# Gate projections spread through the RWKV inverse, a split first input chunk, and sums moved between engines

## The chip, the cores and the metric

One Trainium2 chip, one of its cores. The metric is the device time of one execution in microseconds (us), from the runs' own counter. A core has five engines with instruction streams of their own: TensorE (PE, matmuls into PSUM), VectorE (DVE), ScalarE (ACT), GpSimd (POOL) and SyncE (SP, which here only starts transfers). They wait for each other by semaphores.

## What is computed

One layer of a hybrid decoder for 256 prompt rows and 8 sample rows, width 1024, float32. Shortened from the reference:

```python
mod = silu(c) @ w_mod + b_mod               # 6 x 1024 columns
sh1, sc1, gt1, sh2, sc2, gt2 = split(mod)
h = rms_norm(x, norm1) * (1 + sc1) + sh1
p = h @ w_in            # q | k | v | rwkv (1792) | gate_a (1024) | gate_b (1024)
o_a = sliding_window_attention(q, k, v)     # 8 query heads, 2 key heads
o_b = rwkv7_mix(p_rw)                       # delta-rule state, 8 heads of 64x64
m = sigmoid(gate_a) * (o_a @ w_pa) + sigmoid(gate_b) * (o_b @ w_pb)
x = x + gt1 * (m @ w_o)
x = x + gt2 * moe(rms_norm(x) * (1 + sc2) + sh2)   # top 4 of 32 experts
```

The recurrence over the 256 prompt rows is done in four chunks of 64 rows; each head and chunk needs the inverse of a triangular 64x64 matrix.

## The kernel before

Everything is kept transposed: 128 features on the partitions, T = 264 rows in the free dimension. A projection of 128 output columns is 8 matmuls of 128x128 by 128x264; in float32 each is two PE instructions, and each has its weight load. Weights come through a ring of six slots of 2 MB (`ring`), later with two more in `arena`.

**Transfers.** SP runs through the list `stream` with the slots of `slots_of`: four loads `modA` (the first 2048 columns of `w_mod`, two rows of 128 each), then input chunks (`win`, 512 columns each) and modulation chunks (`mod`) in turn, then `pa`, `pb`, `wo` and the last two `mod`. Before each reuse of a slot SP waits until PE has used it (`chunk_used`, which knows the order of PE's work by the list `a_order`). From `AFTER_RWKV` on it waits for the end of the carry (`carry_evac` 5). Behind the list come the experts' weights, 6 chunks of 2 MB for each of 32 experts (line 394).

**Setup.** PE turns x (line 837), adds up its squares over the partitions (831), makes scale and shift (855, 861); DVE forms `HT`, the normalised, scaled and shifted input (1550 to 1567), and PE starts input chunk 0 (909). Then for each pair: a modulation chunk (869, 875) and an input chunk (900).

**Gates.** Input chunks 5 to 7 and a quarter of 8 are 13 columns of the two gates. They are not worked off in one go: `gates(n)` in PE's stream (line 890) issues the next n of 104 steps (13 columns of 8 steps), at hand-chosen places where PE would wait. Each column has a PSUM bank from `GATE_BANK`; ACT takes it with `gates(b)` (557).

**Attention.** Four blocks `g4`: `scores` (986), softmax on DVE and ACT (1676 to 1685, 621), `probabilities` (transposes, 1000; ACT copies, 627) and `values` (1012). Then the sample rows' attention and state update, mostly on DVE (1697 to 1730).

**Inverse.** PE forms the triangular matrices (1129); DVE masks them (1759, 1761, 1764). Levels `i` of 1, 2, ..., 32 rows double the inverse: in each, PE makes Y (1156), ACT copies it (679), PE makes the corrections (1164, 1168), DVE adds them (1788, 1791), for two halves n. Keys by values (1176) and the product with the inverse (1185) follow, and then the carry: products over all heads and chunks (1202, 1205, 1209, 1210) and the state over four chunks (1219, DVE 1812 and 1814), output products (1225, 1226, 1229), the end state (1236).

**Rest.** Normalisation, mixer (1272), output projection (1304), router, and the experts (1359 to 1436).

## Time and profile before

| | |
|---|---|
| median of 3 runs | 1295.73 us (1293.49 to 1296.33) |
| profiled execution, its own time | 1295.52 us |
| its span, first to last instruction | 1293.7 us |
| busy: PE, PE weight load, DVE | 1243.3, 619.1, 446.1 us |
| busy: ACT, POOL | 296.8, 53.3 us |
| mean granted PE clock | 0.99 of 2.4 GHz |
| HBM read, written | 463.91 MB, 5.09 MB |

A busy time is the time in which at least one instruction of the engine ran. For PE it says little of how full the array is, since matmuls are pipelined. The idle time of an engine matters only where others wait for it. The chain of waits follows the last instruction back to what released it, step by step.

### The profile page before, as it was taken

Reading aid. Unit: us, or ns where it says so; the run is one execution under the profiler, and the core shown is the slowest. Engines: PE = TensorE matmul, PEld = TensorE weight load, DVE = VectorE, ACT = ScalarE, POOL = GpSimd, SP = SyncE. Lnnn points to the kernel's source line nnn. Section 1 sums busy time; section 2 is a strip of 40 time slices with the busy share of each in tenths; the row PEclk is TensorE's granted clock in tenths of the full one; section 3 lists DMA queues with packets and bytes.
Section 4 is the critical chain, followed back from the end, with each engine's and each line's share of the span. In section 5 each row is a group of like instructions: output and inputs, shape, how many; then the busy total and the mean of one; then the engine's idle time right before and its main releaser. Section 6 shows DMA issues by size and latency. Waiting matters only on the chain.

```text
span 1293.7 us, 21059 instructions
## 1 busy us (share of the span) xinstructions
PE 1243.3 (96%) x8371; PEld 619.1 (48%) x8371; DVE 446.1 (34%) x1035; ACT 296.8 (23%) x548; POOL 53.3 (4%) x67
## 2 busy tenths in 40 slices
PE   7999998899999999999999999999999999999998
PEld 5787786788743333333333333333333333333343
DVE  2145747546353222233322223332222223332232
ACT  3012441220232221122222112222211122221211
POOL 0010622200000000000000000000000000000000
PEclk9999998999999999999999999999999999999999
DMA  9976352148689999999999999999999999999995
GB/s 362 364 255 249 115 158 76 36 149 308 252 354 404 427 428 428 429 430 428 427 429 429 428 429 429 428 428 428 429 428 429 429 428 427 429 429 427 429 427 226
DMA packets 55613, 467.14 MB, mean 361 GB/s; under 512 B 5142, under 2 KB 7450, under 8 KB 29691
## 3 DMA queue, kind: packets, MB, share of 16 engines
q1 hardware_dynamic: 53354, 461.07, 85.9%
q0 software_dynamic: 1664, 5.20, 1.5%
q8 instruction: 40, 0.66, 0.2%
q10 hardware_dynamic: 544, 0.13, 0.0%
q14 instruction: 11, 0.08, 0.0%
HBM read 463.91 MB, written 5.09 MB: 363 GB/s over the span
## 4 chain that ended last, share of the span: by engine, by line
PE 77%; DMA 18%; ACT 2%; DVE 2%; issue 1%; SPq 0%; DVEq 0%
PE ps L1415 26%; DMA ring<-in_w 15%; PE ps L1436 14%; PE ps L1359 6%; PE ps L900 5%; PE ps L1384 4%; PE ps L890 4%; DMA ring<-in_w_in 2%; PE ps L1304 2%; PE ps L1272 2%; PE ps L1424 2%; PE ps L1366 1%; ACT PT L766 1%; PE ps L909 1%; PE ps L869 1%
## 5 line engine op out<-in xcount | busy, mean ns | idle before, releaser
L1415 PE MATMUL ps<-ring,PT 128*64 128x512 f32 x1536 | 337.3, 593 | 7.1 <-DMA ring<-in_w 6.8
L1970 DVE TENSOR_TENSOR SQ<-ps,SQ 128x528 f32<-128x528 f32 x124 | 79.1, 700 | 590.9 <-PE ps L1384 590.9
L1415 PEld LDWEIGHTS ps<-ring,PT 128*64 128x64 f32 x1536 | 109.8, 137 | 227.9 <-issue 210.4
L1436 PE MATMUL ps<-ring,PT 128*64 128x512 f32 x768 | 170.1, 595 | 0.0
L761 ACT COPY HT<-ps 128x512 f32<-128x512 f32 x62 | 33.3, 589 | 369.4 <-PE ps L1415 369.4
L1415 PE MATMUL ps<-arena,PT 128*64 128x512 f32 x512 | 113.5, 593 | 1.7 <-DMA arena<-in_w 1.7
L1436 PEld LDWEIGHTS ps<-ring,PT 128*64 128x64 f32 x768 | 53.2, 137 | 99.8 <-issue 99.8
L1359 PE MATMUL ps<-XR,PT 128*64 128x512 f32 (+1 forms) x384 | 94.1, 607 | 0.1
L1415 PEld LDWEIGHTS ps<-arena,PT 128*64 128x64 f32 x512 | 37.6, 137 | 74.0 <-issue 68.7
L1384 PE MATMUL ps<-PT 64*128 64x264 f32 x496 | 71.7, 408 | 0.0
L900 PE MATMUL ps<-HT,ring 128*128 128x264 f32 x304 | 69.3, 388 | 0.0
L774 ACT COPY PT<-ps 128x512 f32<-128x512 f32 x31 | 18.2, 587 | 199.7 <-PE ps L1436 199.7
L1384 PEld LDWEIGHTS ps<-PT 64*128 64x128 f32 x496 | 42.5, 185 | 41.4 <-issue 25.1
L900 PEld LDWEIGHTS ps<-HT,ring 128*128 128x128 f32 x304 | 57.3, 190 | 10.4 <-issue 0.8
L1436 PE MATMUL ps<-arena,PT 128*64 128x512 f32 x256 | 56.7, 595 | 0.0
L890 PE MATMUL ps<-HT,ring 128*128 128x264 f32 x208 | 53.4, 412 | 0.6 <-ACT arena L557 0.6
L890 PEld LDWEIGHTS ps<-HT,ring 128*128 128x128 f32 x208 | 40.9, 202 | 10.0 <-issue 2.7
L1359 PEld LDWEIGHTS ps<-XR,PT 128*64 128x64 f32 (+1 forms) x384 | 21.7, 134 | 49.6 <-issue 49.6
L761 ACT ACT_TABLE_LOAD x30 | 38.5, 1283 | 1.0 <-issue 0.5
L764 ACT ACT_TABLE_LOAD x30 | 38.5, 1283 | 0.5
L1424 PE MATMUL ps<-cst,HT 128*128 128x128 f32 x256 | 35.0, 280 | 0.7 <-ACT HT L787 0.7
L1932 DVE TENSOR_SCALAR PT<-cst,PT 128x128 f32<-128x128 f32 (+1 forms) x96 | 27.1, 339 | 24.8 <-DVE PT L1983 22.4
(457 smaller groups left out, 1154.8 us busy)
## 6 DMA issues: line engine op xcount, KB each, us to landing
ring<-in_w SPq DMA_DIRECT2D x144, 2048.0 KB, 27.1
arena<-in_w SPq DMA_DIRECT2D x48, 2048.0 KB, 27.7
ring<-in_w_mod SPq DMA_DIRECT2D x12, 2048.0 KB, 15.0
ring<-in_w_in SPq DMA_DIRECT2D x9, 2048.0 KB, 14.6
ring<-in_w_o SPq DMA_DIRECT2D x2, 2048.0 KB, 11.1
ring<-in_w_pa SPq DMA_DIRECT2D x1, 2048.0 KB, 9.1
ring<-in_w_pb SPq DMA_DIRECT2D x1, 2048.0 KB, 8.4
bias_rows<-bias_by_distance POOLq DMA_DIRECT2D x1, 1536.0 KB, 13.8
```

The source lines that it names most:

```text
L761: act.copy(UR[:, h, :].rearrange("p (f r) -> p f r", f=4), ps[:, 2 + h, :].rearrange("p (r f) -> p f r", f=4)).then_inc(sem["ur_evac"], 1)
L764: act.activation(US_, UG, ACT.Sigmoid, scale=1.702).then_inc(sem["us_ready"], 1)
L890: last = mm(ps[:, GATE_BANK[b], 0:T], w[:, k, s * P:s * P + P], HT[:, k, :], start=(k == 0), stop=(k == KD - 1))
L900: last = mm(bank[:, 0:T], w[:, k, s * P:s * P + P], HT[:, k, :], start=(k == 0), stop=(k == KD - 1))
L1272: last = mm(ps[:, k % 4, 0:T], w[:, i, k * P:k * P + P], (OA, OT)[q][:, i, :], start=(i == 0), stop=(i == 3))
L1359: last = mm(ps[64 * s:64 * s + 64, 0, :], OH[0:rows_in, n, :], XR[0:rows_in, n, s * 512:s * 512 + 512], start=(n == 0), stop=(n == 2))
L1384: last = mm(ps[:, bank + s, 0:T], YS[64 * s:64 * s + 64, p * P:p * P + P], GT[64 * s:64 * s + 64, :], start=True, stop=True)
L1415: last = mm(ps[64 * lin:64 * lin + 64, 2 + hh, :], XG[:, k % 4, k // 4, :], slot_tile(slot, c)[:, k % 2, lin * FE + hh * 512:lin * FE + hh ...
L1424: last = tr(ps[:, 2 + hh, f * P:f * P + P], UR[:, hh, f * P:f * P + P], ID)
L1436: last = mm(ps[64 * hh:64 * hh + 64, 4, :], AC[:, f, :], slot_tile(slot, c)[:, f % 4, hh * 512:hh * 512 + 512], start=(f == 0), stop=(f == ...
L1932: ins = v.tensor_scalar(OG[0:nt, n, :], IO2[0:nt, :], POSM[0:nt, n, col], GATE[0:nt, n, col], ALU.is_equal, ALU.mult)
L1970: v.tensor_tensor(YA[:, p::4, :], ps[:, bank:bank + 2, 0:T], YA[:, p::4, :], ALU.add).then_inc(sem["comb_used"], 1)
```

## The change

It has these parts:

- The four `modA` loads now hold first the scale columns (two loads of four rows of 128), then the shift columns; input chunk 0 is queued between them, in two loads of 1 MB. Input chunk 7 is queued behind modulation chunk 9 instead of ahead of it.
- The sums of squares for the first norm are made on ACT and DVE by rows (`accum_out`), and PE spreads the reciprocal roots over the partitions with three matmuls.
- Input chunk 0 is multiplied with the scaled, unshifted input (`SQ`); the shift vectors go through the same weights in 32 small matmuls, and DVE adds the result. `HT` with the shift is made for the later chunks.
- The scaling of the attention weights by their sums moves from DVE to ACT. The sample's queries are turned by two matmuls instead of eight.
- The 104 gate steps: 8 as before ahead of attention; 48 instead of 72 within it; 16 as before from there to level 1, at other places (4, 5, 4, 3 instead of 10, 4, 2); 12 instead of none in levels 2 to 5; 8 as before beside the product with the inverse; 12 instead of none in the carry. The columns get other PSUM banks.
- Keys by values are made in level 1 and copied there.
- Of the sample state's update a part moves from DVE's sample section into levels 1 to 4, and the sample output from the levels to behind level 5; the copy `OS` goes ahead of an addition.
- In the carry the pairs of products that add up in one bank are issued as two loops, first all of one kind and then all of the other; the output products go ahead of the state loop.

The core of the diff:

```diff
-        stream = [("modA", wmod, j) for j in range(4)]
-        for j, m in zip(range(5), (4, 5, 6, 7, 8)):
+        stream = [("modA", wmod, 0), ("modA", wmod, 1), ("win", win, 0), ("modA", wmod, 2), ("modA", wmod, 3), ("mod", wmod, 4)]
+        for j, m in zip(range(1, 5), (5, 6, 7, 8)):
             stream += [("win", win, j), ("mod", wmod, m)]
-        stream += [("win", win, 5), ("win", win, 6), ("win", win, 7), ("mod", wmod, 9), ("win", win, 8),
+        stream += [("win", win, 5), ("win", win, 6), ("mod", wmod, 9), ("win", win, 7), ("win", win, 8),
                    ("pa", None, 0), ("pb", None, 0), ("wo", wo, 0), ("wo", wo, 1), ("mod", wmod, 10), ("mod", wmod, 11)]
 
 
-        slots_of = [0, 1, 2, 3] + [4, 0, 1, 2, 3, 0, 1, 2, 0, 1] + [0, 1, 0, 1, 1, 0, 3, 2, 1, 4, 5]
+        slots_of = [0, 1, 4, 2, 3] + [0, 1, 2, 3, 0, 1, 2, 0, 1] + [0, 1, 0, 0, 1, 0, 3, 2, 1, 4, 5]
...
-        GATE_BANK = [4, 5, 7, 5, 7, 5, 7, 5, 7, 0, 3, 3, 2]
+        GATE_BANK = [4, 5, 7, 5, 7, 0, 7, 1, 3, 7, 3, 7, 0]
...
-                    sp.dma_start(row_pairs(slot), src[:, 2 * j:2 * j + 2, 0:2 * D]).then_inc(sem[f"ring{slot}"], 16)
+                    cols = slice(D, 2 * D) if j < 2 else slice(0, D)
+                    sp.dma_start(half_rows(slot), src[:, 4 * (j % 2):4 * (j % 2) + 4, cols]).then_inc(sem[f"ring{slot}"], 16)
+                elif (kind, j) == ("win", 0):
+                    sp.dma_start(ring[:, slot, 0:4, :], src[:, 0:4, 0:512]).then_inc(sem["ld_win0"], 16)
+                    sp.dma_start(ring[:, slot, 4:8, :], src[:, 4:8, 0:512]).then_inc(sem[f"ring{slot}"], 16)
...
+            def row_squares(n):
+
+                return act.activation(SQf[:, 0:D], XR[:, n, :], ACT.Square, accum_out=st[:, 70 + n:71 + n])
+
+            chain(row_squares(0))
             for k in range(KD):
-                chain(act.copy(XT[:, k, :], group()))
-                act.activation(SQ[:, k, :], XT[:, k, :], ACT.Square).then_inc(sem["a_evac"], 1)
+                act.copy(XT[:, k, :], group()).then_inc(sem["a_evac"], 1)
+            row_squares(1).then_inc(sem["ss_done"], 1)
             act.wait_ge(sem["ms_ready"], 1)
-            act.activation(RS[:, :], RS[:, :], ACT.Sqrt).then_inc(sem["sqrt_done"], 1)
+            act.activation(st[:, 70:73], st[:, 70:73], ACT.Sqrt).then_inc(sem["sqrt_done"], 1)
...
+                act.wait_ge(sem["att_sum"], g4 + 1)
+                for g in range(4):
+                    ins = act.mul(Pm[:, g, 0:J], Pm[:, g, 0:J], st[:, 8 + g:9 + g])
+                ins.then_inc(sem["att_p"], 1)
...
+                if i == 1:
+                    act.wait_ge(sem["u0_done"], 2)
+                    for n in range(2):
+                        for s in range(2):
+                            ins = act.copy(ZU[:, 8 * n:8 * n + 8, CH:P].rearrange("p (g s d) k -> p s g d k", s=2, d=2)[:, s],
+                                           ps[:, 3 + 4 * s, n * 256:n * 256 + 256].rearrange("p (g d k) -> p g d k", g=2, d=2))
+                        ins.then_inc(sem["u0_evac"], 1)
+                if i == 4:
+                    gates(9)
...
+            first_modulation(0)
+            pe.wait_ge(sem["ms_ready"], 2)
+            for n, (t0, nt) in enumerate(TILES):
+                last = mm(ps[:, 6, t0:t0 + nt], st[0:nt, 70 + n:71 + n].broadcast_to([nt, P]), ID[0:nt, 0:nt], start=True, stop=True)
+            last.then_inc(sem["ss_done"], 1)
+            first_modulation(1)
+            first_modulation_transposed(0)
...
+            def first_part(s, ks):
+
+                for k in ks:
+                    mm(ps[:, 4 + s, 0:T], w[:, k, s * P:s * P + P], SQ[:, k, :], start=(k == 0), stop=(k == KD - 1))
+
+            pe.wait_ge(sem["ld_win0"], 16)
+            for k in range(4):
+                pe.wait_ge(sem["h1_ready"], k + 1)
+                for s in range(4):
+                    first_part(s, [k])
+            weights("win", 0)
+            pe.wait_ge(sem["h1_ready"], KD)
+            first_part(0, range(4, KD))
+            first_modulation(2)
+            first_part(1, range(4, KD))
+            first_part(2, range(4, KD))
+            first_modulation(3)
+            first_part(3, range(4, 6))
+            first_modulation_transposed(1)
+            first_part(3, range(6, KD))
+            pe.wait_ge(sem["h1_ready"], KD + 1)
+            for k in range(KD):
+                for s in range(4):
+                    last = mm(ps[32 * s:32 * s + 32, 2, 2 * P:3 * P], SHT[:, k, :], w[:, k, s * P:s * P + P], start=(k == 0), stop=(k == KD - 1))
+            last.then_inc(sem["mod_a_used"], 1)
+            pe.wait_ge(sem["mod_a_evac"], 3)
+            tr(ps[:, 3, 2 * P:3 * P], MR, ID).then_inc(sem["setup_t"], 1)
 
             modulation(4)
+            pe.wait_ge(sem["h1_ready"], KD + 2)
+            pe.wait_ge(sem["setup_ready"], 2)
             project([1])
...
-            for h in range(HQ):
-                s = h % 2
-                last = mm(ps[:, 2 + s, NS * (h // 2):NS * (h // 2) + NS], II[64 * s:64 * s + 64, :], PTv[64 * s:64 * s + 64, h // 2, NP:T],
+            for s in range(2):
+                last = mm(ps[:, 2 + s, 0:4 * NS].rearrange("p (a b) -> p a b", b=NS), II[64 * s:64 * s + 64, :], PTv[64 * s:64 * s + 64, 0:4, NP:T],
...
             scores(0)
-            gates(12)
+            gates(8)
             pe.wait_ge(sem["qs_evac"], 1)
             scores(1)
-            gates(12)
+            gates(8)
             probabilities(0)
             scores(2)
             values(0)
-            gates(16)
+            gates(8)
             probabilities(1)
             scores(3)
             values(1)
-            gates(16)
+            gates(8)
+            pe.wait_ge(sem["att_max"], 3)
+            gates(3)
             probabilities(2)
             gates(1)
             values(2)
-            gates(12)
+            gates(10)
             probabilities(3)
-            gates(3)
+            gates(2)
             values(3)
...
-            gates(10)
+            gates(4)
...
-                    gates(4)
+                    gates(5)
...
-                if n == 0:
-                    gates(2)
+                gates(4 - n)
+            pe.wait_ge(sem["f_evac"], 8)
+
+            def keys_values(n):
+
+                for h, par in quads:
+                    u, q = 8 * n + h, other(h, par)
+                    col = 4 * n * CH + in_group(h) * CH
+                    last = mm(ps[64 * q:64 * q + 64, 7 if q != par else 3, col:col + CH], half(KR, par)[:, u, 0:CH],
+                              half(Vr, par)[:, u, :], start=True, stop=True)
+                last.then_inc(sem["u0_done"], 1)
...
+                if i == 1:
+                    pe.wait_ge(sem["f_evac"], 9)
+                    keys_values(0)
+                elif i == 2:
+                    pe.wait_ge(sem["u0_evac"], 2)
+                    gates(1)
+                else:
+                    gates(1)
...
+                    if n == 0:
+                        if i == 1:
+                            keys_values(1)
+                        else:
+                            gates(2)
...
             last.then_inc(sem["carry_done"], 1)
+            gates(2)
             for h, c in allu:
                 last = mm(head_chunk(4, h, c), rows_of(XZW, h, c, 0, CH), rows_of(Br, h, c, 0, CH), start=True, stop=True)
             last.then_inc(sem["carry_done"], 1)
-            pe.wait_ge(sem["f_evac"], GATES)
+            gates(2)
+
+            def first_in_bank(h, c):
+
+                return h < 2 and c < 2
+
+            def last_in_bank(h, c):
+
+                return h >= HQ - 2 and c >= NCHUNK - 2
+
+            pe.wait_ge(sem["f_evac"], 11)
             for h, c in allu:
-                mm(head_chunk(2, h, c), rows_of(Br, h, c, 0, CH), rows_of(XZW, h, c, CH, P), start=True, stop=False)
-                last = mm(head_chunk(2, h, c), rows_of(Kr, h, c, 0, CH), rows_of(Vr, h, c, 0, CH), start=False, stop=True)
+                mm(head_chunk(2, h, c), rows_of(Kr, h, c, 0, CH), rows_of(Vr, h, c, 0, CH), start=first_in_bank(h, c), stop=False)
+            pe.wait_ge(sem["dr_ready"], 2)
+            gates(1)
+            for h, c in allu:
+                last = mm(head_chunk(2, h, c), rows_of(Br, h, c, 0, CH), rows_of(XZW, h, c, CH, P), start=False, stop=last_in_bank(h, c))
             last.then_inc(sem["carry_done"], 1)
-            pe.wait_ge(sem["dr_ready"], 2)
+            gates(2)
             pe.wait_ge(sem["mc_ready"], 2)
-            for c in range(NCHUNK):
...
+            for h, c in allu:
+                mm(head_chunk(4, h, c), rows_of(Vr, h, c, 0, CH), rows_of(KR, h, c, CH, P), start=first_in_bank(h, c), stop=False)
+            gates(1)
+            for h, c in allu:
+                last = mm(head_chunk(4, h, c), rows_of(XZW, h, c, CH, P), rows_of(NR, h, c, CH, P), start=False, stop=last_in_bank(h, c))
+            last.then_inc(sem["o_done"], 1)
+            pe.wait_ge(sem["f_evac"], 12)
+            for c in range(1, NCHUNK):
+                pe.wait_ge(sem["g_ready"], c)
                 for h in range(HQ):
                     s, hp = h % 2, h // 2
-                    out = head_chunk(4, h, c)
-                    mm(out, rows_of(XZW, h, c, CH, P), rows_of(NR, h, c, CH, P), start=True, stop=False)
-                    last = mm(out, rows_of(Vr, h, c, 0, CH), rows_of(KR, h, c, CH, P), start=False, stop=True)
-                for h in range(HQ if c else 0):
+                    last = mm(ps[64 * s:64 * s + 64, 7, hp * CH:hp * CH + CH], MC[64 * s:64 * s + 64, hp, c, :],
+                              G4[64 * s:64 * s + 64, c - 1, hp, :], start=True, stop=True)
+                last.then_inc(sem["gm_done"], 1)
+                for h in range(HQ):
                     s, hp = h % 2, h // 2
                     last = mm(ps[64 * s:64 * s + 64, 6 if c < 3 else 3, (c - 1) % 2 * 256 + hp * CH:(c - 1) % 2 * 256 + hp * CH + CH],
                               G4[64 * s:64 * s + 64, c - 1, hp, :], ZR[64 * s:64 * s + 64, hp, c, 1, :], start=True, stop=True)
                 last.then_inc(sem["o_done"], 1)
+                gates(2 if c == 1 else 1)
...
+            def sample_state(part):
+
+                hs = slice(16 * (part % 2), 16 * (part % 2) + 16)
+                if part < 2:
+                    chain(v.tensor_tensor(T2[:, hs, :], sa[:, hs].unsqueeze(2).broadcast_to([P, 16, CH]),
+                                          VEC[:, 2, :].unsqueeze(1).broadcast_to([P, 16, CH]), ALU.mult))
+                elif part == 2:
+                    chain(v.tensor_tensor(S0[:, hs, :], S0[:, hs, :], T2[:, hs, :], ALU.add))
+                else:
+                    done(v.tensor_tensor(S0[:, hs, :], S0[:, hs, :], T2[:, hs, :], ALU.add), "smp_step", 1)
...
-                    sample_output(i - 1)
+                    sample_state(i - 1)
+            for part in range(4):
+                sample_output(part)
```

## Rows read from the trace of the kernel before

**Rows 1.** The page, part 2: transfer rate in 40 slices of 32.3 us.
```profile
GB/s 362 364 255 249 115 158 76 36 149 308 252 354 404 427 428 428 429 430 428 427 429 429 428 429 429 428 428 428 429 428 429 429 428 427 429 429 427 429 427 226
```

**Rows 2.** Chain of waits, whole span: start, length, engine, written tile, line.
```profile
362.10 2.97 PE ps L1359 x12
...
940.79 33.45 DMA ring<-in_w
...
999.55 33.42 DMA ring<-in_w
```

**Rows 3.** The same chain, setup.
```profile
34.70 14.50 PE ps L909 x64
...
51.09 14.44 PE ps L900 x64
```

**Rows 4.** Answer on line 358: issues (ns, first and last), transfers to landing.
```profile
L358 SPq DMA_DIRECT2D ring<-in_w_mod x4: 407/466/470, 3.5 to 5.0; - x4
...
DMA to landing us min/median/max: 10.0/16.8/24.3
```

**Rows 5.** Timeline of the setup: start, us, engine, line, operation.
```profile
20.20 1.28 ACT L544 ACT_TABLE_LOAD   x1
...
22.36 5.25 PE L855 MATMUL ps<-ring,cT 128*32 128x128 f32 x173
```

**Rows 6.** Timelines of projections and attention, DVE, ACT and POOL.
```profile
86.25 2.52 DVE L1588 SCALAR_TENSOR_TENSOR arena<-arena,PC,PT 128x264 f32<-128x264 f32 x6
...
133.00 0.36 ACT L597 COPY ring<-ps 128x256 f32<-128x256 f32 x1
...
146.86 4.70 DVE L1685 TENSOR_SCALAR ring<-ring,st 128x128 f32<-128x128 f32 x4
...
148.87 2.41 POOL L459 TENSOR_TENSOR PT<-ring 128x1024 f32<-128x1024 f32 x1
...
164.73 1.22 DVE L1678 TENSOR_REDUCE st<-ring 128x4 f32<-128x1028 f32 x1
...
166.20 0.51 ACT L621 ACTIVATE ring<-ring,st 128x257 f32<-128x257 f32 x1 [2.23 <-DVE st L1679]
```

**Rows 7.** Chain of waits from the sample's attention to level 1.
```profile
184.15 1.02 PE ps L1039 x8
...
199.85 2.30 DVE XR L1717
202.17 0.23 DVE XR L1719
...
203.09 5.84 PE ps L890 x16
...
209.49 1.13 PE ps L890 x4
...
220.44 0.69 PE ps L1156 x32
```

**Rows 8.** Busy time by stretch: engines (count), granted clock, DMA share, GB/s.
```profile
204.00:206.00 2.00, 2.00 (x6) 1.53 (x5) 1.83 (x6) 0.00 (x0) 0.00 (x0) 0.50 0.02 4
```

**Rows 9.** Chain of waits in the levels; PE's pauses of 120 to 290 us.
```profile
236.08 0.86 PE ps L1168 x30
...
242.35 2.32 issue
...
245.40 1.51 PE ps L1168 x30
...
250.67 0.52 PE ps L1176 x28
...
PE ps L1164 <- issue: 5.2, 4, 2.3
```

**Rows 10.** Chain of waits in the carry.
```profile
259.53 0.88 PE ps L1205 x60
...
272.31 3.76 PE ps L900 x16
```

More of the change, by code:

```diff
@@ L901, in project @@
                         last.then_inc(sem["a_done"], 1)
-            w = weights("win", 0)
-            for s in range(4):
-                bank = group()
-                for k in range(KD):
-                    if s == 0:
-                        pe.wait_ge(sem["h1_ready"], k + 1)
-                    last = mm(bank[:, 0:T], w[:, k, s * P:s * P + P], HT[:, k, :], start=(k == 0), stop=(k == KD - 1))
-                last.then_inc(sem["a_done"], 1)
+            w = ring[:, slots_of[STREAM_AT["win", 0]], :, :]
+            def first_part(s, ks):
[23 more added lines that the diff above has]
+            tr(ps[:, 3, 2 * P:3 * P], MR, ID).then_inc(sem["setup_t"], 1)
             modulation(4)
+            pe.wait_ge(sem["h1_ready"], KD + 2)
+            pe.wait_ge(sem["setup_ready"], 2)
             project([1])
```

162 lines of the change are left out of this document (79 added, 83 removed).

## The prediction

> **What bounds the kernel now.** I read the chain of waits over the whole span first. Its late part repeats two pieces: 33.45 us of waiting for an expert's weights at 940.79 and again at 999.55, so two experts take 58.76 us, 29.4 each [rows 2]. The transfer rate in forty slices is 427 to 429 GB/s from about 420 us on [rows 1]. So the end is set by the stream of expert weights, and that stream can't start before the ring slots come free, which TensorE (PE) decides: its first expert matmuls stand at 362.10 [rows 2]. Nothing in front of them is full for long: the slices before 300 us move 36 to 364 GB/s [rows 1]. What PE saves ahead of 362 us therefore moves the whole stream, and the end, by the same amount. The reader is to see two regimes: transfer bound behind, PE's own order in front.
>
> I then read the front in pieces: the setup, where PE waits for the first input chunk and starts it at 34.70 [rows 3]; attention and gates; the sample's attention; the inverse's levels; the carry. In each the question is whether PE works or waits.
>
> **Setup.** Before, four modulation loads and then the input chunk are queued; the first lands at 3.54 + 10.0 = 13.5, the last modulation load at 5.0 + 24.3 = 29.3, the chunk just before 34.70 [rows 3, 4]: 5.3 us per 2 MB. After, the same bytes come in another order: scale columns 13.5 and 18.8, chunk halves 21.5 and 24.1, shift columns 29.4 and 34.7, modulation 4 at 40.0, input chunk 1 at 45.3. The pieces are narrower (4 KB a row for modulation), which I take at the same rate.
> The row norms leave PE (eight 264-wide sums) for two 1024-wide squares on ScalarE (ACT); a table load of 1.28 [rows 5] and small instructions follow, and they should be ready near 17.7, before the second load lands. A modulation quarter is 64 matmuls at 5.25/173 us, 1.94 [rows 5]. So 18.8 + 1.94, then a copy, two transposes and four small VectorE (DVE) instructions at 0.23 [rows 7] and a first scaled row at 0.42 (2.52 for six) [rows 6], some 2.2 together: PE starts the chunk near 23.0. From there it owes the chunk, 14.5 [rows 3], two shift quarters, the shift pass and modulation 4 (4 x 1.94 = 7.8), and about 1.3 for two transposes with their copies: 23.0 + 23.6 = 46.6. The shift quarters are wanted at 32 and 38 and have landed. Final rows, 8 x 0.42 = 3.4 on DVE, lie under the shift pass and modulation 4; four copies out of PSUM with two small ones, near 2 in all, lie beside modulation 4. Chunk 1 landed at 45.3. It started at 51.09 before [rows 3]: **-4.5**. Bounds: 0 if cover fails everywhere, -5.8 if PE only waits for the landing.
>
> **Queries for the sample.** Eight small products become two wide ones, in front of the first scores: by the 64-wide instructions of the levels, 30 in 0.86 [rows 9], four instructions instead of sixteen save 0.4, by the wide steps' latency up to 1: **-0.7**. Bounds 0 and -1.
>
> **Attention.** Gate steps between scores and values fall from 72 to 48. A step is a pass like the 32 of the first chunk, 14.50/32 = 0.453 [rows 3], 0.46 with the change over, so 24 steps are 11.0 us off PE, if the softmax is still hidden. The scaling by the row sum moves from DVE to ACT: four 128x256 at 0.36 [rows 6] are 1.44 behind the exponentials. On DVE they took up to 4.70, because each waited out a GpSimd (POOL) instruction of 2.41 beside it [rows 6]. The wide softmax is then 1.22 (add) + 1.22 (max) + 0.2 + 4 x 0.51 + 0.3 + 1.44 = 6.4 [rows 6]. Its covers on PE: for the third block scores 1.1, values 0.6 and 11 steps (5.1), 6.8; for the fourth 11 steps and values, 6.9. Both hold by under 0.5. A DVE instruction caught behind POOL costs up to 2.4, once or twice in the first half. I take 0.7 of new waits: **-10.3**. Bounds: -11.0, and -6 with two such catches. PE's new wait for the third maximum has eight gate steps in front of it and should be free. In SP's queue modulation 9 now goes ahead of input chunk 7; both have 15 us or more before use, so nothing.
>
> **Sample's attention, up to the first products.** The chain from 184.15 is DVE's. The copy of the sample output goes ahead of the 2.30 us state addition at 199.85 [rows 7]; the outer product behind it goes to the levels. PE had then ten gate steps: 5.84 + 1.13 [rows 7] where ten cost 4.6, since the granted clock was 0.50 (1.2 GHz) at 204 to 206 [rows 8], after PE had waited for that copy. After: copy at 199.9 + 0.2, addition to 202.4, four copies to 203.2, with PE's four steps inside. The products start at 203.3 instead of 209.49 + 1.13 = 210.6 [rows 7]: **-7.3**. Bounds: -5 if a further DVE instruction comes in front, -7.5.
> Between there and level 1 five, four and three steps stand where four and two did: 12 against 6, 2.8 us, of which 0.9 falls into old waits for the masks: 11.7 instead of 9.8 (210.6 to 220.44): **+1.9**.
>
> **Levels.** They run from 220.44 to 250.67 [rows 7, 9], 30.2 us. PE's own work there is three blocks of 64 instructions a level, 1.4 to 1.8 each (30 in 0.86 [rows 9]), about 4.5, and 1.5 less in the last level: 21.0. The rest is waiting: for the evacuations by ACT, low clock, and pauses with no releaser, 5.2 us on one line, the largest 2.32 [rows 9]. Now 12 steps (5.5) and the keys-with-values (1.3, about 64 instructions) are put in those places: 21.0 + 6.8 = 27.8 if every pause goes. The sample state on DVE is again 1.22 per level, and DVE's 4.1 per level stays under PE's 5.9. **-2.4**. Bounds: -2.4, and +3 if the 5.2 of pauses stay.
> The pauses are where PE meets many 64x64 instructions. The largest fall where another transfer runs (the w_pa load, the state's store). By the Trainium skill (Runtime: NRT & Kernel Launch, Instruction fetch mechanics) the sequencer fetches instructions in blocks of 256 by DMA while the current block runs, mostly hidden. Taken so, longer gate instructions in between would hide it, and the whole sum would be 1273.1.
> The w_pa load is not gone: it waits for gate 11, which now ends in the carry, and its 2 MB land 9 us later, well before use but amid dense instructions. I add **+2.5** in levels and carry together for pauses that stay or move; bounds 0 and 7.
>
> **Level 5 to carry.** From 250.67 the keys-with-values (0.52 at their end) and their copies stood before the next product [rows 9]; both are gone from here: **-1.5**, and no less than -1 since that 0.52 and two ACT copies go. DVE gets four sample-output instructions (4 x 1.22 = 4.9) and 1.6 of bonus here, where PE has 7.2 with 8 steps: just covered; if not, +1.
> **Carry.** From 259.5 to 272.31 before [rows 10], 12.8. Twelve steps go in, 5.5. Some 3 of it covers waits: three times PE stood while DVE formed the next state (two instructions of about 0.45, by the 0.42 of rows 6), and once in a pause. About 15.2: **+2.4**. Bounds +1 and +5.
>
> **Sum.** -4.5 - 0.7 - 10.3 - 7.3 + 1.9 - 2.4 + 2.5 - 1.5 + 2.4 = -19.9. The first expert matmuls move from 362.1 to 342.2. The profiled execution took 1295.52 for a span of 1293.7; the median is 1295.73. 1295.52 - 19.9 = **1275.6**.
>
> **Rivals.** *A, the softmax becomes the bound* (chance 0.15): with ACT scaling, PE waits in each of three blocks some 1.5 to 2 more. For it: margins under 0.5. Against: DVE is relieved by up to 4.7. 1295.5 - 15 = 1281.
> *B, the pauses in the levels persist or grow* (0.15): 5.2 stays, the moved load adds 2 to 3: 1283.
> *C, the gates only change place* (0.04): total PE work is hardly less, so if waits come back elsewhere, 1293 to 1297, within 0.2%. Against it: PE stood idle for 2.32 in one pause alone [rows 9], and gates now stand there.
> *D, setup gains more and no pause stays* (0.10): 1295.5 - 24 = 1271.
> *E, slower* (0.03): PE's clock. At 244 to 248 level blocks went at 1.2 GHz, 1.51 against 0.86 for 30 instructions [rows 9]. Were the grant low from level 1 to the end of the carry, 45 us of work would grow by some 70%, 32 us: 1307. It decides from 28 us of such work on. Against it: lower grants lasted 3 to 7 us, and there are fewer gaps now. The Trainium skill (TensorE: Matmul & The Clock Gate, Part 1) says that idleness throttles and activity releases, which speaks for fewer drops.
>
> **Numbers.** My sum has 0.53. 0.2% is about what this kernel's measurement can tell from nothing. Faster is the forecast with A, B and D, 0.93; C gives 0.03 to same and 0.01 to slower: same 0.03, slower 0.04. The range runs from below D to above B: 1267 to 1286, and all but C, E and the tails of the others lie in it; its width is the bounds of attention (5), pauses (7), carry (4) and setup (4), not all at once.
>
> **What would show it.** Input chunk 1 starting near 46.6; last values of attention 15 us earlier; the first products after the sample's copies with no low clock in front; levels of 5.9 us with no pause over 1 us; first expert matmuls at 342; expert periods unchanged at 29.4. Wrong if attention shows PE waiting for ACT, if pauses move to the carry, or if the expert stream does not move along.

## The result

The changed kernel took 1282.23 us (median of 4 runs, 1281.01 to 1283.18) beside 1294.61 us for the kernel before (1291.26 to 1296.33, 4 runs): ratio 0.9901, 95% interval 0.9886 to 0.9916. Faster, as forecast, and inside the range, but by some 12 to 13 us where the sum had 19.9. The profiled execution took 1282.87 us for a span of 1281.0, 12.7 less than the span before.

The page, part 2, in 40 slices of 32.0 us, and the whole chain of waits of the changed kernel:

```profile
GB/s 356 367 286 249 101 104 70 101 294 305 222 347 428 426 430 427 428 430 427 428 429 428 428 429 428 428 429 428 428 429 428 428 429 428 428 429 426 429 428 222
...
347.30 2.97 PE ps L1440 x12
...
928.06 33.46 DMA ring<-in_w
986.84 33.44 DMA ring<-in_w
```

The two regimes are as before [rows 1, 2]. Two experts take 986.84 - 928.06 = 58.78 us, and the waits for their weights stand 12.73 earlier than the 940.79 of [rows 2]; the end moved with them. The first expert products stand at 347.30, 14.8 earlier than 362.10. So the front (all that PE does ahead of its first expert product) gave 14.8, not 19.9, and 2.1 were lost again behind 347 us. Setup, in the chain:

```profile
14.88 3.57 PE ps L871 x64
...
19.41 1.93 PE ps L871 x64
...
23.75 9.14 PE ps L934 x40
...
47.34 4.69 PE ps L926 x20
```

L871 is the first modulation, 64 matmuls a quarter: the first quarter took 3.57, the second 1.93. L926 is the second input chunk, 47.34 against 51.09 [rows 3]: -3.75. The sample's attention to level 1, in the chain, and below it busy time by stretch (the number behind the engines is the granted clock):

```profile
169.99 1.02 PE ps L1089 x8
...
186.60 3.82 PE ps L916 x8
190.43 2.84 PE ps L1179 x64
...
195.70 1.91 PE ps L1179 x64
...
203.12 1.09 PE ps L1216 x64
```

```profile
186.00:188.00 2.00, 2.00 (x7) 1.64 (x8) 2.00 (x1) 0.49 (x1) 0.00 (x0) 0.50 0.01 4
...
190.00:192.00 2.00, 2.00 (x33) 1.64 (x36) 0.00 (x0) 0.00 (x0) 0.00 (x0) 0.50 0.00 0
```

L916 are gate steps, two instructions each. Eight of them (four steps) took 3.82 at 186.60 at a granted clock of 0.50 (1.2 GHz, "the half clock" below) and 1.98 at 198.53, 233.12 and 236.14; the first 64 products (L1179) took 2.84, the next 64 only 1.91. Levels and carry, in the chain ("issue" is a pause for which the profile names no releaser):

```profile
201.59 1.53 PE ps L916 x6
...
207.30 0.89 issue
...
211.47 0.55 issue
...
228.36 0.64 PE ps L916 x2
...
230.08 1.09 PE ps L916 x4
...
232.25 0.88 PE ps L1249 x30
233.12 1.98 PE ps L916 x8
...
238.12 1.14 PE ps L1266 x62
...
250.20 1.73 issue
...
257.55 3.76 PE ps L926 x16
```

The gate groups of 1, 2, 3 and 4 steps took 0.64, 1.09, 1.53 and 1.98: 0.445 a step, and 0.19 for each group whatever its size. The start of the experts:

```profile
354.00:356.00 2.00, 2.00 (x6) 0.51 (x4) 0.88 (x4) 0.43 (x1) 0.21 (x1) 0.50 0.64 274
```

```profile
352.34 15.65 PE ps L1496 x64
```

The first 64 expert products ran partly at the half clock and took 15.65; in the run of the best version, below, they took 13.95.

### The profile page after: what moved, and what is told of

Its sections match the earlier page's. It is cut to its first block, busy times and chain, and to the rows that moved or that the text cites. A ratio compares the mean times of both kernels' runs of the same rounds, so it can differ in the third digit from the quotient of the medians.

```text
span 1281.0 us, 21166 instructions
## 1 busy us (share of the span) xinstructions
PE 1237.6 (97%) x8414; PEld 607.5 (47%) x8414; DVE 443.1 (35%) x1041; ACT 298.5 (23%) x558; POOL 53.0 (4%) x67
## 4 chain that ended last, share of the span: by engine, by line
PE 76%; DMA 16%; DVE 4%; ACT 3%; issue 1%; SPq 0%; POOL 0%; DVEq 0%
PE ps L1496 27%; DMA ring<-in_w 16%; PE ps L1517 14%; PE ps L1440 6%; PE ps L926 5%; PE ps L1465 4%; PE ps L1385 2%; PE ps L1353 2%; PE ps L916 2%; PE ps L1505 2%; PE ps L1447 1%; ACT PT L789 1%; PE ps L934 1%; PE ps L895 1%; PE ps L871 1%
## 5 line engine op out<-in xcount | busy, mean ns | idle before, releaser
L926 PE MATMUL ps<-HT,ring 128*128 128x264 f32 x304 | 69.3, 388 | 0.2 <-issue 0.2
L926 PEld LDWEIGHTS ps<-HT,ring 128*128 128x128 f32 x304 | 57.3, 190 | 10.7 <-issue 1.1
L916 PE MATMUL ps<-HT,ring 128*128 128x264 f32 x208 | 55.9, 410 | 0.0
L916 PEld LDWEIGHTS ps<-HT,ring 128*128 128x128 f32 x208 | 38.1, 195 | 8.1 <-issue 1.4
L784 ACT ACT_TABLE_LOAD x30 | 38.5, 1283 | 1.0 <-issue 0.5
L787 ACT ACT_TABLE_LOAD x30 | 38.5, 1283 | 0.5
```

What stands on the lines that cost most here:

```text
L784: act.copy(UR[:, h, :].rearrange("p (f r) -> p f r", f=4), ps[:, 2 + h, :].rearrange("p (r f) -> p f r", f=4)).then_inc(sem["ur_evac"], 1)
L787: act.activation(US_, UG, ACT.Sigmoid, scale=1.702).then_inc(sem["us_ready"], 1)
L916: last = mm(ps[:, GATE_BANK[b], 0:T], w[:, k, s * P:s * P + P], HT[:, k, :], start=(k == 0), stop=(k == KD - 1))
L926: last = mm(bank[:, 0:T], w[:, k, s * P:s * P + P], HT[:, k, :], start=(k == 0), stop=(k == KD - 1))
```

## The experiments

All were timed in five rounds; ratios are to the kernel before, run beside them. Each has one trace. "Attention" below is the time from the second input chunk's start to the sample's transposes behind the last values (before: 184.15 - 51.09 = 133.1; changed: 169.99 - 47.34 = 122.65).

**The changed kernel again** (no edit).

> The changed kernel itself once more, unedited, as the measure for the experiments beside it and for how far its profile repeats. Theory 1 (its first trace, with a mean granted clock of 0.995 and no half clock near 128, was a lucky execution; the experiments' own traces of the same attention code show the half clock at 124 to 132): more runs give a median 0.5 to 2 us above 1282.23, runs at a lower mean clock are the longer ones by some 0.8 us for each 0.001, and the stretch from the second chunk to the sample's transposes takes 123 to 126 us in place of 122.6. Theory 2 (the trace is typical): median within 0.5 us of 1282.2, clock 0.995, the stretch 122.6.

1285.29 us (1281.48 to 1286.83, 6 runs), ratio 0.9916 [0.9901, 0.9932] with before at 1295.78. The first theory holds in its direction: the first trace was a lucky execution. Its size was too small, since the median rose by 3.1 us where it had 0.5 to 2 (by the ratios it is 1.9, and the two intervals overlap). Over the ten executions of this kernel, six with a mean granted clock of 0.994 to 0.996 took 1281.0 to 1283.2 us, and four with 0.991 to 0.993 took 1283.9 to 1286.8. Attention took 123.3, with the half clock at 124 to 132 that the first trace lacks; the kernel before has one at 128 to 136. The half clock also followed the carry's pause, in the chain and by stretch:

```profile
251.41 1.75 issue
```

```profile
254.00:256.00 2.00, 2.00 (x32) 1.62 (x32) 0.23 (x1) 0.00 (x0) 0.00 (x0) 0.69 0.03 8
256.00:258.00 2.00, 2.00 (x20) 1.20 (x17) 0.62 (x2) 0.00 (x0) 0.00 (x0) 0.50 0.00 0
```

**Setup alone** (the kernel before with the setup part of the diff, its stream order included).

> The kernel before with the setup part of the change alone: first chunk in two loads without its shift, the split first modulation, the mean squares by row, and the stream order that these need; attention, sample, inverse and carry are those of before. Theory 1 (the setup's gain passes through whole): the second chunk's products start at 47.3 in place of 51.09, as in the changed kernel, every later mark is 3.7 to 3.8 us earlier, and the median is 3.8 us below before, ratio 0.997. Theory 2 (the gain is lost at the first wait of attention, whose softmax on VectorE and ScalarE sets the pace): the mark stands at 47.3, but the last values end less than 2 us earlier than 184.15 and the time is 0 to 2 us lower. What is left between this run and the changed kernel, 8.6 us by theory 1, is the worth of the rest of the change.

1292.82 us beside 1295.3, ratio 0.9975 [0.9963, 0.9987], 3.2 us (1.7 to 4.8) by the ratio. The second chunk started at 48.4 in its trace, and attention took 133.1 as before: the gain passes through attention whole. Over all traces with this setup code that start lies between 47.2 and 48.6, before it was 51.1 and 51.3, so the setup is worth 2.5 to 4.1. Its trace also warns of single traces: 2.6 us were gained at the end of attention, but 6.1 at the first expert products, though the code between is that of before. Those 3.5 us are the spread between executions.

**Gate steps ahead of the sample's wait.**

```diff
             token_rows(6)
             token_rows(7)
+            pe.wait_ge(sem["row_evac"], 6)
+            gates(4)
             pe.wait_ge(sem["smp_att"], 4)
...
             pe.wait_ge(sem["row_evac"], 8)
-            gates(4)
```

> The changed kernel with the four gate steps at 186.60 moved ahead of the wait for the sample's five copies (the wait for token rows' sixth copy goes with them), so that TensorE has work while VectorE copies from 185 to 189. Theory 1 (the low clock from 186 to 192 follows the light work ahead of it, and the four steps stood behind the idle time at half rate): the four steps take 1.98 us as at the full clock and not 3.82, they lie under VectorE's copies, the first 64-row products run at 1.91 us for 64 and not 2.84, level 1 starts 2 to 3 us earlier than 203.12, and the time falls by 2 to 3 us. Theory 2 (the clock falls here for another reason, or VectorE's copies, which end at 189.06, set the start of the first products): the first products start 0 to 0.5 us earlier than 190.43, the clock row still shows 0.50 in 187:190, and the time is within 0.7 us of the changed kernel.

1284.02 us, ratio 0.9908 [0.9889, 0.9927]: not to be told from the changed kernel. My first theory falls, and its picture with it. In the chain:

```profile
187.28 2.96 PE ps L916 x8
190.24 0.36 PE ps L1149 x4
...
192.00 1.05 PE ps L1180 x29
```

TensorE was not idle at the new place. The steps now stand ahead of L1149, which VectorE's last four copies need, and delay them; in the changed kernel they run beside these copies. The steps still met the half clock (2.96 for eight instructions). The products started 21.0 us after the last values' transposes, 20.4 in the changed kernel.

**Scaling of the attention weights back on VectorE**, in all blocks, and in all but the first.

```diff
-                v.reciprocal(st[:, 8:12], st[:, 8:12]).then_inc(sem["att_sum"], 1)
+                chain(v.reciprocal(st[:, 8:12], st[:, 8:12]))
+                for g in range(4):
+                    ins = v.tensor_scalar(Pm[:, g, 0:J], Pm[:, g, 0:J], st[:, 8 + g:9 + g], None, ALU.mult)
```

> The changed kernel with the scaling of the softmax weights back on VectorE, as before (four multiplications behind the reciprocal in place of ScalarE's). Theory 1 (ScalarE's four multiplications of 1.28 to 1.71 us a block are what TensorE waits for: 2.5 us of its idle time in attention and 0.3 more stand behind them): the weights are ready sooner, the last values end 1 to 2.5 us earlier than 169.99, and the time falls by as much. Theory 2 (VectorE is the fuller engine, and its multiplications behind GpSimd's instructions take 2 us and more, as the 4.70 us one did before): the last values end 2 us or more later than 169.99, and the time rises by 2 to 5 us. Theory 3 (either engine is as late as the other): within 1 us.

> The changed kernel with the softmax scaling on ScalarE for the first block of attention alone, and on VectorE for the other three. With all four on VectorE only the first block's multiplication was slow (4.69 us for four, behind GpSimd's instructions, TensorE idle 2.32 us); with all four on ScalarE TensorE idled 2.5 us in four waits of 0.3 to 0.9 us. Theory 1 (each wait is local, and no other wait takes its place): TensorE's idle time ahead of these transposes falls to 0.9 us or less, and the stretch to the sample's transposes is 1.2 to 1.8 us shorter than in the changed kernel at the same clock. Theory 2 (VectorE's own chain is as full, and its sinks and copies come later by as much): idle time only moves to the score or value products, under 0.5 us of gain.

All blocks: 1286.37 us, ratio 0.9932 [0.9917, 0.9947], attention 126.1. All but the first: 1284.0 us (1281.44 to 1289.2), ratio 0.9906 [0.9892, 0.9921], attention 127.1. The changed kernel's waits, and the multiplications in the timelines of the two runs, one fence each:

```profile
PE ps L1048 <- ACT ring L641: 2.5, 4, 0.9
```

```profile
143.44 2.42 POOL L458 TENSOR_TENSOR ring<-ring,arena 128x1056 f32<-128x1056 f32 x1
143.93 4.69 DVE L1789 TENSOR_SCALAR ring<-ring,st 128x128 f32<-128x128 f32 x4
148.67 0.66 PE L1044 MATMUL ps<-cst,ring 128*128 128x128 f32 x4 [2.32 <-DVE ring L1789]
```

```profile
148.80 2.21 DVE L1789 TENSOR_SCALAR st<-st 128x4 f32<-128x4 f32 x1
153.01 3.17 DVE L1798 TENSOR_SCALAR ring<-ring,st 128x128 f32<-128x128 f32 x4
```

On VectorE the multiplications that fall beside GpSimd's 2.4 us instructions (143 to 156) were slow, and so was a small one ahead of them: four elements a partition took 2.21. With the first block's scaling on ScalarE the second was caught, and TensorE idled 3.6 for it. But not all of that is the scaling's: the small one was also caught with all scaling on ScalarE, in the traces of the merged groups, the paired sums and the late load below, where TensorE idled 1.7 to 1.8 and attention took 126.0, 126.0 and 124.7. From the first of them:

```profile
148.83 2.20 DVE L1782 TENSOR_SCALAR st<-st 128x4 f32<-128x4 f32 x1
154.36 0.66 PE L1048 MATMUL ps<-cst,ring 128*128 128x128 f32 x4 [1.71 <-ACT ring L641]
```

So the traces show which instruction waits, but the length of attention alone doesn't tell the engines apart, and neither does the time: both intervals overlap that of the changed kernel's second set. Both of my readings of single waits were too local. From 155 us on GpSimd has many short instructions instead of those; the best version below takes VectorE in the last two blocks, and its trace has none of these waits.

**The same gate steps in seven groups fewer.**

```diff
                 elif i == 2:
                     pe.wait_ge(sem["u0_evac"], 2)
-                    gates(1)
+                    gates(3)
                 else:
-                    gates(1)
+                    gates(3)
...
-                        else:
-                            gates(2)
```

> The changed kernel with the same gate steps in fewer groups: three steps at once in each of levels 2 to 5 in place of one and two, and in the carry 4, 4, 2, 1, 1 in place of 2, 2, 1, 2, 1, 2, 1, 1. Seven groups fewer. Theory 1 (each group of full-width products between 64-row products costs a fixed 0.18 us, as the groups of 1 to 12 steps show: 0.64, 1.09, 1.53, 1.98 and 5.54 us): TensorE loses 7 x 0.18 = 1.3 us, and if no wait opens in the levels the time falls by 1.0 to 1.3 us. Theory 2 (the spread groups hide waits for VectorE's copies in the levels): TensorE idles between the halves of a level for 0.3 us or more each, and the time rises by 0.5 to 2 us. Theory 3: the two cancel, within 0.5 us, with both to be seen in the trace.

1283.21 us (1279.38 to 1286.37), ratio 0.9899 [0.9880, 0.9918]; not to be told from the changed kernel by time. Its profiled execution was the longest of its six. The traces tell more: from level 1 to the product with the inverse 27.8 us instead of 29.1 in both traces of the changed kernel, for four groups fewer and pauses of 1.2 against 1.4 and 1.2. That is 1.3 where 4 x 0.19 gives 0.76, so the price of a group fits only roughly. In the carry the pause grew instead, and the half clock followed (chain):

```profile
251.26 2.77 issue
...
254.72 2.06 PE ps L916 x4
```

**The load of `w_pa` kept back.**

```diff
+                if kind == "pa":
+                    sp.wait_ge(sem["carry_evac"], 5)
```

> The changed kernel with the 2 MB load of the first output-side matrix kept back until the carry's fifth copy, some 15 us later, so that no large transfer is under way in the carry. Theory 1 (TensorE's pause of 1.73 us at 250.20, for which the trace names no wait, is an instruction fetch held up behind that load; before, the pause of 1.77 us at 222.40 stood behind the same load): the pause shrinks to 0.6 us or less or is gone, and the second part of the last chunk starts 1.1 to 1.7 us earlier, at 255.9 to 256.4 in place of 257.55; the time falls by that or, if the matrix is now late, less. Theory 2 (the pause is one of the regular fetches of this many short instructions and has nothing to do with the load): it stays at 1.5 us or more, at the same place in the instruction stream, time unchanged within 0.5 us. A cost: the product with that matrix may wait for it; then a wait on its ring slot shows.

1281.77 us (1278.89 to 1283.14), ratio 0.9889 [0.9874, 0.9903], beside 0.9916 [0.9901, 0.9932] for the unedited one run with it: the medians are 3.5 us apart, but the intervals touch, and beside the first four executions (1282.23) it is 0.5. What the edit does is read from the trace. By stretch, the changed kernel first (the last two numbers are the transfer share and GB/s):

```profile
248.00:250.00 2.00, 2.00 (x90) 1.71 (x89) 0.00 (x0) 0.00 (x0) 0.00 (x0) 1.00 0.74 299
250.00:252.00 2.00, 0.27 (x10) 0.13 (x6) 0.85 (x2) 0.00 (x0) 0.00 (x0) 1.00 0.03 10
```

```profile
248.00:250.00 2.00, 2.00 (x88) 1.59 (x79) 0.00 (x0) 0.00 (x0) 0.00 (x0) 1.00 0.00 0
250.00:252.00 2.00, 1.94 (x35) 1.51 (x30) 0.85 (x2) 0.00 (x0) 0.00 (x0) 1.00 0.04 8
```

```profile
250.67 0.06 issue
...
256.35 3.76 PE ps L927 x16
```

The pause of 1.73 to 1.75 is 0.06. From the carry's first product (238.58) to the last chunk it takes 17.8 us instead of 19.4, and instead of the 21.0 of the second trace, where the half clock came behind the pause. In both traces of the changed code without this load in the carry (this one and the best version's) the half clock did not come there. The matrix, landed 9.5 us after its issue at 256.8, made nobody wait.

**The carry's sums in pairs again.**

```diff
-                mm(head_chunk(2, h, c), rows_of(Kr, h, c, 0, CH), rows_of(Vr, h, c, 0, CH), start=first_in_bank(h, c), stop=False)
...
+                mm(head_chunk(2, h, c), rows_of(Br, h, c, 0, CH), rows_of(XZW, h, c, CH, P), start=True, stop=False)
+                last = mm(head_chunk(2, h, c), rows_of(Kr, h, c, 0, CH), rows_of(Vr, h, c, 0, CH), start=False, stop=True)
```

> The changed kernel with the carry's two sums made again as before, each unit's two products right behind one another, in place of one pass of 64 products and, behind gate steps, a second pass of 64. Theory 1 (an accumulating product waits for the one ahead of it into the same place: before, the pairs took 3.04 and 3.7 us where four separate passes take 4 x 1.14 = 4.56 us): the four passes take 6.5 to 6.9 us, and the last chunk's second part starts 2.0 to 2.4 us later than 257.55. Theory 2 (in before the pairs were slow for their dependence on VectorE, not for the pairing): the passes take 4.6 to 5 us and the time is within 0.5 us.

1285.37 us (1283.7 to 1285.56), ratio 0.9918 [0.9905, 0.9930]: no difference by time. (The edit also moves one of the passes behind a wait and a gate step that it stood ahead of.) In the chain the first 64 pairs stand between two groups of gate steps of 1.53 us, at 244.89 and 249.19, and took 249.19 - 244.89 - 1.53 = 2.77 us where two separate passes take 2.28: 0.5 dearer, where the first theory had 1.1 for these and as much for the other sum. The second 64 ran into the pause and the half clock and can't be read.

**No gate steps in the levels** (all twelve behind the last level).

```diff
-                else:
-                    gates(1)
...
+            gates(12)
             for n in range(2):
                 pe.wait_ge(sem["xx_ready"], 2 * (len(LEVELS) - 1) + n + 1)
```

> The changed kernel with its twelve gate steps inside levels 2 to 5 taken out of the levels and made in one piece between the last level and the products behind it; the keys with the values stay in level 1. It measures what the filling is worth. Theory 1 (the steps fill waits for ScalarE's and VectorE's copies): TensorE idles in the levels for most of what it saves; eight groups fewer save 8 x 0.18 = 1.4 us, the idle time is over 3 us, and the stretch from level 1 to the products behind the levels grows by 2 us or more, time up by 2 us or more. Theory 2 (TensorE's own work sets the pace of the levels and the copies keep up by themselves): idle time under 1.4 us and the time falls by up to 1.4 us.

1287.67 us, ratio 0.9938 [0.9924, 0.9952]. Level 1 to the product with the inverse: 32.6 instead of 29.1. The block itself took 5.54. The waits of the levels, the largest three of four (the last is 0.2, on ScalarE):

```profile
PE ps L1228 <- issue: 3.5, 5, 1.2
PE ps L1215 <- issue: 1.4, 2, 0.7
PE ps L1228 <- ACT ring L696: 0.5, 2, 0.3
```

The filling is worth what the first theory said, but not for the reason it gave. Of 5.6 us of idle time 4.9 are pauses without a releaser and only 0.7 the copies by ScalarE. With the steps in place the pauses were 1.4.

**More products ahead of the first expert.**

```diff
             gather()
+            for _ in range(3):
+                mm(ps[:, 6, 0:T], ONE, HT[:, 0, :], start=True, stop=True)
             pe.wait_ge(sem["xr_evac"], 1)
```

> The changed kernel with six more products on TensorE, whose results nobody reads, in the two waits ahead of the first expert (three behind the first gather, three behind its transposes; 0.22 us each). Theory 1 (the half clock at 352 to 358, seen in four of six traces of this code, follows these waits): the granted clock stays at 1.00 up to 360, the first 64 expert products take 13.95 us in place of 15.65, and the time falls by 1 to 2 us. Theory 2 (it follows what lies further back, the small matrices from 336 on and the wait at the mean square, or comes and goes by itself): the trace shows 0.50 there again or at 338 to 344, and the time is unchanged or up by the 0.2 us by which the extra products outlast the waits.

1284.17 us, ratio 0.9898 [0.9883, 0.9913]: no gain beside the changed kernel's. In this trace the half clock came at 342 to 348, ahead of the waits that the edit fills, and the first 64 expert products took 13.88. That proves nothing for the edit: in six of the ten traces of this code without it they took 13.95 too, and in four 15.65. What sets the half clock off there stays open.

**The late load in the kernel before** (the same two lines).

> The kernel before, with nothing of the change, and the same 2 MB load kept back until the carry's fifth copy; before, it was issued at 218.47 and ran through the first levels. Theory 1 (a load beside dense 64-row products lengthens the fetch of instructions, but in the kernel before they are also dense enough to outrun it alone): of the 6.8 us of TensorE's pauses without a named wait in the levels and the carry, the one behind the load (1.77 us at 222.40) shrinks to 0.7 us or less, those at 236 to 251 (0.86, 2.32 and 0.52 us) stay, and the time falls by 1 to 2.5 us. Theory 2 (all pauses are the load's doing): all shrink, 4 us or more lower. Theory 3 (the load mattered only for the changed kernel's order): no pause changes, time within 0.6 us.

1294.6 us beside 1296.24, ratio 0.9984 [0.9975, 0.9993], 2.1 us by the ratio (0.9 to 3.2). Chain, and GpSimd's timeline:

```profile
225.53 0.71 issue
...
241.03 2.05 issue
```

```profile
235.74 1.16 POOL L505 DMA_DIRECT2D out_wkv_sample<-XR  x2
```

In place of the 1.77 behind the load the first pause was 0.71, 3 us later, but one of 0.86 followed 4 us behind it, and the six pauses of the levels are 6.1 us together, where five were 5.9 before. The levels took 28.0 instead of 30.2: the half clock that the trace of before shows in them [rows 9] was absent here. So the time agrees with the first theory, and its mechanism only for the one pause. Pauses of 0.71, 0.86 and 0.86 stood with nothing transferring: the 64-row products make pauses of that size by themselves. The 2.05 did not stand alone: GpSimd had issued the store of the sample's state at 235.74 (the line above), and it ran into the pause. The 2.32 of the kernel before [rows 9] stood beside the same store, issued there at 237.32, which this edit leaves where it is. The prediction had named both transfers; only the load was followed up.

All fourteen traces fit this. Between 190 and 265 us fourteen of TensorE's pauses without a releaser were longer than 1.2 us, 1.34 to 2.77, and each had the load of `w_pa` or that store under way in the pause or the 2 us ahead of it. Without one of the two no pause was longer than 1.17. Only the load was ever moved, so for the store this is a meeting in time and not a shown cause; pauses of 0.99 and, in the kernel before, 0.72 met its start.

**The best version**: late load, groups merged, scaling on VectorE in the last two blocks.

> Three edits of the changed kernel together: the 2 MB load kept back until the carry's fifth copy (the run of it alone gave 1281.77 beside 1285.29), the gate steps in seven groups fewer (1283.21 alone), and the softmax scaling of the last two blocks on VectorE (of all but the first it was no gain: the second block's took TensorE 3.6 us of idle time). Theory 1 (they add up): 3.5 us from the load, 1 us from the groups, 0.5 to 1.3 us from the scaling, median 1279 to 1281. Theory 2 (the groups' gain was noise, or with fewer fillers a fetch of instructions opens a pause again): median 1281 to 1283, the load's gain alone. The levels take 27.8 us or less from level 1 to the products behind them in place of 28.9 to 29.0, and the carry's part up to the last chunk 17.8 us or less.

1279.17 us (1277.67 to 1282.14), ratio 0.9872 [0.9856, 0.9889] with before at 1297.01. In the chain:

```profile
246.09 0.91 issue
...
252.61 3.76 PE ps L929 x16
...
349.04 13.95 PE ps L1494 x64
```

Attention took 121.9 against 123.3 in the trace of the changed kernel with the same half clock at 124 to 132; level 1 to the product with the inverse 28.2; the carry to the last chunk 17.6, with a pause of 0.91 again where the merged groups leave six passes of 64-row products almost unbroken. It beats the kernel before clearly. Beside the changed one its interval stays below the 0.9901 to 0.9932 of the second set of runs, but not below that of the first four (0.9886 to 0.9916), and it overlaps that of the late load alone, so what merging and scaling add to the load is not shown by time.

## Why the prediction was right, and where its sum was off

**Regimes.** Right. What PE saved ahead of the first experts moved the transfer stream, less the 2.1 below; the periods stayed at 29.4. All fourteen traces, of all versions, bear it out: the end of the first 64 expert products lies anywhere from 363.0 to 381.1, and the span ends 912.6 to 913.2 us behind it.

**Setup**, -4.5 forecast, -3.75 measured. The landings and the work from the chunk's start on were right (23.75 to 47.34 is 23.6, as forecast). Off was the quarter at 1.94: the first took 3.57, so the chunk started at 23.75 and not at 23.0.

**Queries and attention**, -11.0 forecast, -10.4 and -9.7 in two traces. Right in mechanism, and the wait taken at 0.7 came to 2.5 and 1.3: ScalarE's scaling. Part of the first trace's gain is a half clock that it didn't have. The six other traces with this attention code gave -9.9 to -7.1; the three lowest are those with an instruction caught beside GpSimd, which the bound of -6 had allowed for. No run took this part or the next back alone; they are read from the chains.

**Sample's attention**, -7.3 forecast, 26.46 to 20.44 = -6.0 measured; **products to level 1**, +1.9 forecast, +2.9 measured. Both misses are one: I expected no low clock in front of the first products. It stayed, 186 to 192, and cost 1.84 on the gate steps and 0.93 on the first products; 0.6 of the first lay under the copies. The traces of the late load and of the best version settle it, since the half clock stayed away there. The late load's stretch and chain:

```profile
188.00:190.00 2.00, 1.69 (x14) 1.30 (x12) 1.93 (x3) 1.07 (x2) 0.00 (x0) 1.00 0.00 0
```

```profile
192.23 1.98 PE ps L1180 x64
```

There the products started 192.23 - 173.01 = 19.2 us after the transposes, -7.2, and level 1 followed 11.8 later, +2.0: both terms as forecast. The work was right, and the condition on the clock failed.

**Levels and carry**, +2.5 forecast with the allowance for pauses, measured -1.1 (30.2 to 29.1) and +5.5 (13.9 to 19.4), +4.4. The term that failed is the price of a gate step. I took 0.46 wherever it stands; a group costs 0.19 besides, and 8 groups in the levels and 8 in the carry are 6.92 us each where I had 5.5: +2.8. The pauses are 3.2, where 2.5 was allowed: near in size, and half of it is the moved load meeting the carry, as feared. Against both, the products themselves came out 1.6 us cheaper than I had them; that is what is left of the sum, not a measurement. The gain in the levels is less sure than -1.1: in the three traces with the old code they took 28.0, 29.1 and 30.2. **Level 5 to carry**, -1.5 forecast, -1.85.

**Sum up to the experts**: -19.9 forecast, -14.8 measured. Missed were group cost 2.8, clock near the first products 2.3, setup 0.75, pauses 0.7 and attention 0.6, 7.1 together; cheaper products (1.6) and level 5 (0.35) gave 2 of it back. **Behind it**, a term the sum lacked, 2.1 us: 1.7 at the first expert (15.65 where before had 13.95, half clock at 352 to 356), and 0.4 in the stream itself, whose first long wait is 32.01 instead of 31.64. The half clock there differs between executions, as does the one at 124 to 132; that this is why the median of this kernel lies at 1282 in one set of runs and at 1285 in another fits the mean clocks, but only one execution of each set has a trace. **The number.** 1282.2 and 1285.3 are inside 1267 to 1286, but far from the 1275.6 of the sum, and the second is near the edge: the wide range held what the sum had missed.

**Rivals.** The time lies nearer to A's 1281 and B's 1283 than to the sum, but mostly for other reasons (group cost, clock). A is half true: waits for ScalarE, 1.3 to 2.6 and not 4.5 to 6. B is true in the carry alone, 1.7. So two of my three signs of being wrong came true in part: PE waited for ACT, and a pause moved to the carry. E did not come about as one long stretch; the short ones that I can price took 4.5 in the first trace (1.84, 0.93, and 15.65 - 13.95 = 1.7). By the Trainium skill (Runtime: NRT & Kernel Launch, Instruction fetch mechanics) the fetch is mostly hidden. If the pauses are the fetch, which no run shows directly, the traces agree for the levels with wide instructions in between (1.2 to 1.4 us) and not without them (4.9).

## What to carry to other kernels

Fill work costs by the group, not only by the step: put it where the engine would stand, in as few pieces as still break up the long runs of short matmuls (without any, the pauses of the levels grew from 1.4 to 4.9 us), and count 0.2 us for each. When instructions are dense, look for large transfers beside them and move those first; it is a two-line edit, worth 1.7 us in the trace here. And judge an edit of a few microseconds by the same stretch in several traces at the same granted clock, since the executions of one unedited kernel differ by 5.8 us, and the shorter ones have the higher mean clock.

## What the runs showed of the hardware

- In all nine traces with the `w_pa` load in the carry, TensorE paused 1.34 to 2.77 us, 5.4 to 8.0 us behind its issue, with no releaser, in eight of them at the same product of the state loop; with the load moved away the pause there was 0.06 us, and 0.91 with the merged groups. The store of the sample's state had such pauses of 1.60, 2.05 and 2.32 beside it in the three traces with the old levels. That it is the fetch of instructions is inferred: the instruction queue moves a 16 KB packet every few microseconds in these stretches, and the pauses grow with the density of short instructions (1.4 against 4.9 us in the levels), but the profile names no releaser.
- In six of those nine the granted clock fell to 0.50 some 3 us after the pause began; in the two without the load it did not.
- A group of 128-row gate steps among 64-row products takes 0.19 us beyond its steps at 0.445 each (0.64, 1.09, 1.53, 1.98 and, for twelve, 5.54).
- The first modulation quarter took 3.57 us for 64 matmuls and the second 1.93, with the granted clock recorded as 1.00 in both. No run here explains the first.
- VectorE instructions of four elements a partition took 2.1 to 2.3 us beside GpSimd's 2.4 us instructions.
